# Feed-forward down products: two row tiles at a time by seven block products instead of eight

## The chip, the cores and the metric

The kernel runs on one core of one Trainium2 chip. The time is the device time of one execution, in microseconds (us). Three runs of the kernel before took 1896.27, 1896.74 and 1897.19 us; their median is 1896.74 us.

## What is computed

256 tokens (two tiles of 128) of width 1024 pass through fourteen stages: eight gated feed-forward layers and six other stages (a pooling mixer, the shared latent keys and values, latent attention, a norm, a mixer of stick-breaking attention and convolution, gated linear attention). Only the feed-forward layers matter here:

```
swiglu(u, wg, wu, wd) = (silu(u @ wg) * (u @ wu)) @ wd        # u 256x1024, wg and wu 1024x2816, wd 2816x1024
```

The hidden width of 2816 is 22 tiles of 128 (`NF`). Everything is float32. The kernel gets the precision out of TensorE by splitting each operand into a rounded high part and the rest (`hi` and `lo`, both in the fp32r format), and it computes each product as three: hi by hi, hi by lo and lo by hi.

## The kernel before, in words

A feed-forward stage (`ffn`, in each engine's program) runs over 22 steps, one per tile of the hidden width. Step f has two parts on TensorE:

- **gate and up** (`gate_up`, `block_of`): 8 blocks of the width by 3 products by 2 (gate, up) = 48 matmuls of 256 columns, into two PSUM banks of `X`; steps alternate between banks 0, 1 and banks 2, 3.
- **down** (`down`, `down_half`): the hidden tile of 128 rows (2 token tiles) against 1024 columns of `wd` (2 halves): 4 banks of `Y` by 3 products = 12 matmuls of 512 columns (one of them in two halves of 256). `Y` gathers all 22 steps.

TensorE runs gate and up of step f, then down of step f-1. All matmuls go through the helper at L1698.

The weights come from memory by SyncE's queue, in order: one 1 MB tile A (gate and up) and one 0.5 MB tile B (down) per step, each double buffered. `load_A` (L401) waits until the tile before last is split, `load_B` (L406) likewise. ScalarE makes the high parts (`split_A` L590, 2048 columns; `split_B` L610, 1024 columns), VectorE the low parts by a subtraction of two SBUF operands (L1105, L1117). Between these, each step has its activation: VectorE scales gate and up by the norm's root out of PSUM (L1257, L1260), ScalarE applies silu (L708), VectorE multiplies (L1267), ScalarE and VectorE split the product (L717, L1270). One stage (`ffn2`, "reuse") needs no scaling and reads gate and up straight from PSUM. The order of each engine's queue is written out by hand in `step`; the last steps are peeled.

At a stage's end `following` starts the next stage's transposes, VectorE adds Y into the residual (`update`; L1176 where there is no second norm). The next stage's first A tiles are split in the last steps: tile a+22 belongs to the next stage. GpSimd has almost nothing to do: powers for the norms (L475, L489) and a few DMAs and memsets.

Of the kernel before, what the change touches and what calls it, by code (L numbers as in the profile page):

```python
# [16 lines left out]
P = 128  # L17
# [9 lines left out]
POOL_REACH = P + 16  # L27
GLA_HEADS, GLA_DV = 4, 256
# [74 lines left out]
def build(nc, wa, wb, x, cols_in, rows_in, ident_in, trig_in, pool_in, penal_in, sb_in, gla_in, gate_in, taps_in,  # L103
# [8 lines left out]
    with ctx:  # L112
# [8 lines left out]
        rawB = [sb(f"rawB{i}", [P, 1024]) for i in range(2)]  # L121
        hiA = [sb(f"hiA{i}", [P, 2048], f32r) for i in range(2)]
        loA = [sb(f"loA{i}", [P, 2048], f32r) for i in range(2)]
        hiB = [sb(f"hiB{i}", [P, 1024], f32r) for i in range(2)]
        loB = [sb(f"loB{i}", [P, 1024], f32r) for i in range(2)]
# [12 lines left out]
        act_s = sb("act_s", [P, 2, TOKENS])  # L138
        act_h = sb("act_h", [P, 2, TOKENS])
        act_hh = sb("act_hh", [P, 2, TOKENS], f32r)  # L140
        act_hl = sb("act_hl", [P, 2, TOKENS], f32r)
# [9 lines left out]
        cqh = sb("cqh", [P, 2, TOKENS], f32r)  # L151
        cql = sb("cql", [P, 2, TOKENS], f32r)
# [56 lines left out]
        root = arena[:, 12000:12000 + TOKENS]  # L209
# [29 lines left out]
        s_mask = s_const[:, 4 * P:4 * P + 384]  # L239
        s_k = rg.take(SB_PAIRS, TOKENS)  # L240
        s_q = rg.take(SB_PAIRS, 2, TOKENS)
# [8 lines left out]
        s_w = rg.take(4, 384)  # L250
# [6 lines left out]
        g_mask = rg.take(8 * P)  # L257
        g_qk = rg.take(GLA_HEADS, 512)
# [8 lines left out]
        g_sm = rg.take(8, P)  # L267
# [37 lines left out]
        out_done = sem("out_done")  # L305

# [50 lines left out]

        def tap(c, j):
            w = COL["conv_w"] + CONV_W * c + j
            return s_pad[:, c, j:j + TOKENS], cols[:, w:w + 1]  # L360
# [30 lines left out]

        HALF = [slice(0, 512), slice(512, 1024)]
# [3 lines left out]
        def _(sp):  # L396
# [6 lines left out]
            def load_B(n, p, first=False):  # L403
                if not first:
                    sp.wait_ge(b_lo, n - 1)
                sp.dma_start(rawB[p][:, :], wb[n]).then_inc(b_loaded[p], 16)  # L406
# [9 lines left out]
            for s in plan:  # L416
                a, b = s["a"], s["b"]
                if s["kind"] == "ffn":
                    peel = 2 if a == 0 else 0
                    for f in range(peel):  # L420
                        if f == 0:
                            load_A(a + 1, (a + 1) % 2, first=True)
                        load_B(b + f, (b + f) % 2, first=True)
                        if f == 0:
                            sp.dma_start(cols[:, KD:NCOL], cols_in[:, KD:NCOL]).then_inc(const_loaded, 16)
                    with sp.Fori(peel // 2, NF // 2) as j:
                        for p in range(2):
                            load_A(a + p + 2 * j, (a + p) % 2)
                            load_B(b + p + 2 * j, (b + p) % 2)
# [23 lines left out]
        def _(pool):  # L453
# [18 lines left out]
            for s in plan:  # L472
# [20 lines left out]
                before_mixer = {"ffn1": ("mla",), "final": ("hyb",), "ffn5": ("gla",)}.get(s["name"], ())  # L493
                if s["late"]:
# [7 lines left out]
                if s["a"] == 0:  # L502
                    load_row(0)
                    pool.wait_ge(a_hi, 4)
# [5 lines left out]
                for k in before_mixer:  # L510
# [15 lines left out]
                    if k == "gla":  # L526
                        pool.wait_ge(a_hi, s["a"] + 8)
                        pool.dma_start(arena[:, 0:20 * P], gla_in).then_inc(phase_loaded[k], 16)
                        pool.dma_start(g_gate, gate_in).then_inc(phase_loaded[k], 16)
                        nc.gpsimd.memset(g_lr[0:32, :], 1.0).then_inc(g_ones, 1)  # L530
                if s["kind"] == "kv":
# [39 lines left out]
        def _(act):  # L571
# [90 lines left out]
            def ffn(s):  # L662
# [29 lines left out]
                split_B(b, b % 2)  # L692

                def step(f, p, first=False, last=False):
                    if first:
                        if a:
                            split_A(a + 2, a % 2, 0)
                        if s["late"]:
                            act.wait_ge(root_psum, s["deferred"] + 1)
                            nc.scalar.activation(root, Y[:, 0, 0:TOKENS], ACT.Copy).then_inc(root_done, 1)  # L700
                        if s["reuse"]:
                            latent_root()
# [2011 lines left out]
```

## Time and profile before

| | us |
|---|---|
| median of three runs (lowest to highest) | 1896.74 (1896.27 to 1897.19) |
| span of the profiled execution, first to last instruction | 1894.6 |
| TensorE busy in it | 1874.1 (99%) |
| VectorE busy | 1229.6 (65%) |
| ScalarE busy | 945.6 (50%) |
| GpSimd busy | 66.1 (3%) |
| moved by DMA | 338.6 MB, 179 GB/s on average |

The profiled execution has its span alone; what lies around it is taken as the difference to the median of the runs, 2.1 us. TensorE's mean granted clock is 0.999. A busy share says how much of the span an engine executed something; the chain that ended last says which engine everything else waited for. In the rows below PE is TensorE's matmuls, DVE is VectorE, ACT is ScalarE, POOL is GpSimd.

### The profile page before, as it was taken

What the parts mean: (1) busy time and instruction counts of PE and PEld (TensorE: products, weight loads), DVE (VectorE), ACT (ScalarE), POOL (GpSimd) and SP (SyncE); (2) the same over time, 40 slices, a digit from 0 to 9 for tenths busy, and PEclk for the clock granted to TensorE, in tenths of its full rate; (3) what the DMA queues carried; (4) which work ended last, traced back from release to release, by engine and by line L of the source; (5) the groups of instructions that cost most, each with busy time, mean ns of one, the idle gap of its engine ahead of it and who ended that gap; (6) DMA issues with size and microseconds to landing.
All of it is one profiled execution on the core that took longest, in us unless ns stands there. A gap on an engine that the chain in (4) does not pass through costs nothing.

```text
span 1894.6 us, 34284 instructions
## 1 busy us (share of the span) xinstructions
PE 1874.1 (99%) x13508; PEld 1745.4 (92%) x13508; DVE 1229.6 (65%) x1654; ACT 945.6 (50%) x1301; POOL 66.1 (3%) x94
## 2 busy tenths in 40 slices
PE   9999999999999999999999999999999999999998
PEld 8999999999998889999999998999999998889998
DVE  5666765675556647666765699765676665877665
ACT  5444544454446636444544457644454446455443
POOL 0000100000000000000100000100010002010000
PEclk9999999999999999999999999999999999999999
DMA  7555455545453245555555443565545453344552
GB/s 282 199 191 184 164 199 199 189 165 207 185 198 134 68 149 215 191 183 194 200 199 198 146 145 111 201 233 199 189 167 203 185 199 126 130 152 178 192 199 100
DMA packets 61505, 338.60 MB, mean 179 GB/s; under 512 B 6976, under 2 KB 7360, under 8 KB 33024
## 3 DMA queue, kind: packets, MB, share of 16 engines
q1 hardware_dynamic: 59472, 330.00, 47.3%
q0 software_dynamic: 1968, 7.70, 1.2%
q8 instruction: 45, 0.74, 0.2%
q14 instruction: 20, 0.16, 0.0%
HBM read 336.62 MB, written 1.05 MB: 178 GB/s over the span
## 4 chain that ended last, share of the span: by engine, by line
PE 93%; DVE 3%; ACT 2%; issue 1%; POOL 1%; DMA 1%; SPq 0%; DVEq 0%; ACTq 0%; POOLq 0%
PE X L1698 55%; PE Y L1698 36%; DMA rawA<-in_wa 1%; ACT hiA L590 1%; PE X L1739 1%; ACT arena L804 0%; DVE arena L1481 0%; DVE xs L1193 0%; DVE h L1200 0%; DVE xl L1145 0%; PE Y L2213 0%; DVE loA L1105 0%; DVE arena L1418 0%; POOL ms_eps L489 0%; PE X L1722 0%
## 5 line engine op out<-in xcount | busy, mean ns | idle before, releaser
L1698 PE MATMUL X<-xh,hiA 128*128 128x256 f32 x2464 | 679.0, 277 | 1.7 <-DVE loA L1091 0.8
L1698 PE MATMUL X<-xl,hiA 128*128 128x256 f32 x2464 | 677.4, 277 | 0.0
L1698 PE MATMUL X<-xh,loA 128*128 128x256 f32 x2464 | 668.9, 277 | 0.0
L1105 DVE TENSOR_TENSOR loA<-rawA,hiA 128x2048 fp32r<-128x2048 f32 x213 | 487.9, 2290 | 265.2 <-ACT hiA L590 265.0
L1698 PEld LDWEIGHTS X<-xh,hiA 128*128 128x128 f32 x2464 | 462.7, 188 | 3.2 <-DVE loA L1091 1.7
L1698 PEld LDWEIGHTS X<-xl,hiA 128*128 128x128 f32 x2464 | 463.3, 188 | 0.0
L1698 PEld LDWEIGHTS X<-xh,loA 128*128 128x128 f32 x2464 | 457.1, 188 | 0.0
L590 ACT ACTIVATE hiA<-rawA 128x2048 fp32r<-128x2048 f32 (+1 forms) x239 | 424.0, 1776 | 46.1 <-PE Y L1698 29.8
L708 ACT ACTIVATE act_s<-act_s 128x256 f32<-128x256 f32 x154 | 64.4, 418 | 427.2 <-DVE act_s L1257 427.2
L1698 PE MATMUL Y<-hiB,act_hh 128*128 128x512 f32 x704 | 275.5, 391 | 0.9 <-DVE act_hl L1270 0.9
L1698 PE MATMUL Y<-hiB,act_hl 128*128 128x512 f32 (+1 forms) x880 | 275.9, 346 | 0.0
L1698 PE MATMUL Y<-loB,act_hh 128*128 128x512 f32 x704 | 275.0, 391 | 0.0
L1117 DVE TENSOR_TENSOR loB<-rawB,hiB 128x1024 fp32r<-128x1024 f32 x180 | 219.3, 1218 | 3.9 <-ACT hiB L610 3.8
L717 ACT ACTIVATE act_hh<-act_h 128x256 fp32r<-128x256 f32 x176 | 73.5, 417 | 284.7 <-DVE act_h L1267 284.7
L1698 PEld LDWEIGHTS Y<-hiB,act_hl 128*128 128x128 f32 x880 | 165.2, 188 | 35.3
L610 ACT ACTIVATE hiB<-rawB 128x1024 fp32r<-128x1024 f32 x181 | 189.1, 1045 | 1.6 <-PE Y L1698 1.5
L1260 DVE TENSOR_TENSOR act_h<-X,arena 128x256 f32<-128x256 f32 x148 | 62.5, 423 | 150.7 <-PE X L1698 150.7
L1698 PEld LDWEIGHTS Y<-hiB,act_hh 128*128 128x128 f32 x704 | 132.2, 188 | 24.6 <-issue 3.3
L1698 PEld LDWEIGHTS Y<-loB,act_hh 128*128 128x128 f32 x704 | 132.2, 188 | 21.1
L1270 DVE TENSOR_TENSOR act_hl<-act_h,act_hh 128x256 fp32r<-128x256 f32 x176 | 74.8, 425 | 85.5 <-ACT act_hh L717 85.5
L1698 PE MATMUL X<-oh,hiA 128*128 128x256 f32 x352 | 97.6, 277 | 0.0
L1698 PE MATMUL X<-ol,hiA 128*128 128x256 f32 x352 | 97.4, 277 | 0.0
(263 smaller groups left out, 2217.8 us busy)
## 6 DMA issues: line engine op xcount, KB each, us to landing
rawA<-in_wa SPq DMA_DIRECT2D x221, 1024.0 KB, 5.4
rawB<-in_wb SPq DMA_DIRECT2D x181, 512.0 KB, 3.5
row_gain<-in_rows POOLq DMA_DIRECT2D x8, 512.0 KB, 6.1
arena<-in_gla POOLq DMA_DIRECT2D x1, 1280.0 KB, 5.8
h<-in_x SPq DMA_DIRECT2D x2, 512.0 KB, 4.0
arena<-in_taps POOLq DMA_DIRECT2D x1, 576.0 KB, 5.7
arena<-in_pool POOLq DMA_DIRECT2D x1, 544.0 KB, 6.6
rawA<-in_wa SPq DMA_DIRECT2D x2, 256.0 KB, 5.9
```

The source lines that it names most:

```text
L590: ins = nc.scalar.activation(hiA[p][:, cut], rawA[p][:, cut], ACT.Copy)
L610: nc.scalar.activation(hiB[p][:, :], rawB[p][:, :], ACT.Copy).then_inc(b_hi, 1)
L708: nc.scalar.activation(act_s[:, p, :], act_s[:, p, :], ACT.Silu).then_inc(silu_done, 1)
L717: nc.scalar.activation(act_hh[:, p, :], act_h[:, p, :], ACT.Copy).then_inc(prod_hi, 1)
L1105: nc.vector.tensor_tensor(loA[p][:, :], rawA[p][:, :], hiA[p][:, :].bitcast(f32), ALU.subtract).then_inc(a_lo, 1)
L1117: nc.vector.tensor_tensor(loB[p][:, :], rawB[p][:, :], hiB[p][:, :].bitcast(f32), ALU.subtract).then_inc(b_lo, 1)
L1260: nc.vector.tensor_tensor(act_h[:, p, :], up, root, ALU.mult).then_inc(up_scaled, 1)
L1270: nc.vector.tensor_tensor(act_hl[:, p, :], act_h[:, p, :], act_hh[:, p, :].bitcast(f32), ALU.subtract).then_inc(prod_lo, 1)
L1698: return say(nc.tensor.matmul(*args, **kw))
L1739: ins = nc.tensor.transpose(dst, src, ident[:, :])
```

## The change

In nine of the eleven pairs of steps (`PAIRS = 9`, the first 18 tiles) the down part of two steps is one product of 2 by 2 blocks (2 token tiles by 2 hidden tiles) with 2 by 2 blocks (2 hidden tiles by 2 column halves). It is done with seven block products in place of eight. This needs four sums of weight blocks (u1 to u4, `sums`) and four sums of activation blocks (r3, s1, s2, r4), which GpSimd makes, and seven PSUM banks (Y0 to Y3, X0 to X2) that are joined once, after the ninth pair, on ScalarE and VectorE. The last four tiles run as before (`left`). Gate and up of a step share one bank now: X3 (X2 for f = 1). The weight buffers rawB, sum_hi and sum_lo hold a pair (2048 columns). `taken` takes gate and up (512 columns) out of PSUM in one instruction. The high and low parts of three raw blocks (1536 columns), of the four weight sums (2048) and of the eight activation blocks (1024) replace the splits of B and of the product. The order of the matmuls: gate and up of 2j, `first_sums(j-1)` (9 matmuls of 512 columns), gate and up of 2j+1, `last_sums(j-1)` (12).

```diff
 # SyncE
+                    def pair_loads(j):
+                        load_A(a + 1 + 2 * j, (a + 1) % 2)
+                        load_A(a + 2 + 2 * j, a % 2)
+                        sp.wait_ge(w_sum_done, pairs + j)
+                        sp.wait_ge(b_lo, b + 2 * j)
+                        for p in range(2):
+                            sp.dma_start(rawB[(b + p) % 2], wb[b + p + 2 * j]).then_inc(b_loaded[(b + p) % 2], 16)
...
+                    load_A(a + NF - 1, (a + NF - 1) % 2)
+                    load_B(b + NF - 2, b % 2)
+                    load_B(b + NF - 1, (b + 1) % 2)
 # GpSimd
+                def weight_sums(j):
...
+                    pool.wait_ge(w_sum_lo, pairs + j)
...
+                    nc.gpsimd.tensor_tensor(sums[:, 0:1024].rearrange("p (a b) -> p a b", b=512), ends, twice, ALU.add
+                                            ).then_inc(w_sum_part, 1)
+                    pool.wait_ge(w_sum_part, 2 * (pairs + j) + 1)
...
+                    nc.gpsimd.tensor_tensor(sums[:, 1024:1536], u3, weight_block(s, "b11"), ALU.add
+                                            ).then_inc(w_sum_part, 1)
+                    pool.wait_ge(w_sum_part, 2 * (pairs + j) + 2)
+                    nc.gpsimd.tensor_tensor(sums[:, 1536:2048], sums[:, 1024:1536], weight_block(s, "b21"), ALU.add
+                                            ).then_inc(w_sum_done, 1)
+                def product_sums(j):
+                    pool.wait_ge(prod_done, NF * s["ffn"] + 2 * j + 2)
+                    blocks = prod.rearrange("p (a b) -> p a b", b=P)
+                    nc.gpsimd.tensor_tensor(blocks[:, 4:6, :], blocks[:, 1:2, :].broadcast_to([P, 2, P]),
+                                            blocks[:, 0:4:3, :], ALU.subtract).then_inc(p_sum_part, 1)
+                    pool.wait_ge(p_sum_part, 2 * (pairs + j) + 1)
+                    nc.gpsimd.tensor_tensor(blocks[:, 6, :], blocks[:, 5, :], blocks[:, 0, :], ALU.subtract
+                                            ).then_inc(p_sum_part, 1)
+                    pool.wait_ge(p_sum_part, 2 * (pairs + j) + 2)
+                    nc.gpsimd.tensor_tensor(blocks[:, 7, :], blocks[:, 2, :], blocks[:, 6, :], ALU.add
+                                            ).then_inc(p_sum_done, 1)
 # ScalarE, the loop and what follows it
+                with act.Fori(1, PAIRS) as j:
+                    product_parts(j - 1)
+                    sum_parts(j - 1)
+                    silu(2 * j, 0)
+                    split_A(a + 2 * j + 2, a % 2)
+                    raw_parts(j)
+                    silu(2 * j + 1, 1)
+                    split_A(a + 2 * j + 3, (a + 1) % 2)
...
+                split_A(a + f + 4, a % 2)
+                silu(f + 3, 1)
+                left_product(3)
 # VectorE
+                def taken(f, p):
...
+                    dve.wait_ge(up_psum, e + 1 + f)
+                    if s["late"]:
+                        wide = root.rearrange("p (a b) -> p a b", a=1).broadcast_to([P, 2, TOKENS])
+                        ins = nc.vector.tensor_tensor(act_sh[:, :, p, :], bank, wide, ALU.mult)
...
+                    ins.then_inc(gate_scaled, 1)
...
+                product(0, 0)
...
+                split_A(a + 2, a % 2)
+                taken(1, 1)
+                raw_low(0)
+                product(1, 1)
+                split_A(a + 3, (a + 1) % 2)
+                with dve.Fori(1, PAIRS) as j:
+                    product_low(j - 1)
+                    sum_low(j - 1)
+                    taken(2 * j, 0)
+                    product(2 * j, 0)
+                    split_A(a + 2 * j + 2, a % 2)
+                    raw_low(j)
+                    taken(2 * j + 1, 1)
+                    product(2 * j + 1, 1)
+                    split_A(a + 2 * j + 3, (a + 1) % 2)
+                f = 2 * PAIRS
...
+                nc.vector.tensor_tensor(Y[:, 1, :], Y[:, 1, :], sums[:, 512:1024], ALU.subtract).then_inc(joint_chain, 1)
...
+                left_product_low(1)
+                left_weights_low(1)
+                taken(f + 2, 0)
...
+                left_weights_low(3)
+                split_A(a + f + 4, a % 2)
+                taken(f + 3, 1)
 # TensorE
-                        pe.wait_ge(prod_done, e - 1 + f)
+                        pe.wait_ge(gate_scaled, e + f)
...
+                def first_sums(j, first=False, last=False):
+
+                    pe.wait_ge(b_lo, b + 2 * j + 2)
+                    pe.wait_ge(p_sum_lo, pairs + j + 1)
+                    joined(X[:, 0, :], prod_block("a11"), raw_block(s, "b11"), first, last)
+                    joined(Y[:, 0, :], prod_block("a12"), raw_block(s, "b21"), first, last)
+                    return joined(Y[:, 1, :], prod_block("r4"), raw_block(s, "b22"), first, last, True).then_inc(b_free, 2)
+
+                def last_sums(j, first=False, last=False):
+
+                    pe.wait_ge(w_sum_lo, pairs + j + 1)
+                    joined(Y[:, 2, :], prod_block("a22"), sum_block(s, "u4"), first, last)
+                    joined(Y[:, 3, :], prod_block("s1"), sum_block(s, "u1"), first, last)
+                    joined(X[:, 1, :], prod_block("s2"), sum_block(s, "u2"), first, last)
+                    joined(X[:, 2, :], prod_block("r3"), sum_block(s, "u3"), first, last, True).then_inc(all_sums_psum, 1)
...
-                down(0, 0, first=True)
-                with pe.Fori(1, NF // 2 - 1) as j:
+                gate_up(2, 0)
+                first_sums(0, True)
+                gate_up(3, 1)
+                last_sums(0, True)
+                with pe.Fori(2, PAIRS) as j:
                     gate_up(2 * j, 0)
-                    down(2 * j - 1, 1)
+                    first_sums(j - 1)
                     gate_up(2 * j + 1, 1)
-                    down(2 * j, 0)
+                    last_sums(j - 1)
```

`joined` is three matmuls of 512 columns (the third in two halves where it is told so). For the stages whose first B tile has an even number, the host swaps the column halves of the even tiles of the pairs. Some arena regions move so that `prod` and `sums` are free in all stages. No other stage's instructions change.

## Rows read from the trace of the kernel before

**Rows 1.** The page: busy time of each engine, and the chain that ended last, by line.

```profile
PE 1874.1 (99%) x13508; PEld 1745.4 (92%) x13508; DVE 1229.6 (65%) x1654; ACT 945.6 (50%) x1301; POOL 66.1 (3%) x94
...
PE X L1698 55%; PE Y L1698 36%; DMA rawA<-in_wa 1%; ACT hiA L590 1%; PE X L1739 1%; ACT arena L804 0%; DVE arena L1481 0%; DVE xs L1193 0%; DVE h L1200 0%; DVE xl L1145 0%; PE Y L2213 0%; DVE loA L1105 0%; DVE arena L1418 0%; POOL ms_eps L489 0%; PE X L1722 0%
```

**Rows 2.** Busy time by engine in 18 steps of stage ffn1 (columns in the first row).

```profile
core 0: us, PE busy (x) PEld busy (x) DVE busy (x) ACT busy (x) POOL busy (x), PEclk, DMA share, GB/s
227.60:375.20 147.60, 147.60 (x1101) 139.63 (x1100) 93.05 (x111) 65.06 (x73) 0.00 (x0) 1.00 0.53 196
```

**Rows 3.** Chain of waits of stage ffn1: start us, us, what; its opening, then its end.

```profile
208.72 5.23 PE Y L1698 x46
...
219.97 2.75 PE Y L1698 x13
222.72 5.46 PE X L1698 x48
...
383.98 5.70 PE Y L1698 x26
```

**Rows 4.** Groups of instructions, every shape apart: TensorE, VectorE and ScalarE in the steps.

```profile
L1698 PE MATMUL Y<-hiB,act_hh 128*128 128x512 f32 x704 | 275.5, 391 | 0.9 <-DVE act_hl L1270 0.9
...
L1105 DVE TENSOR_TENSOR loA<-rawA,hiA 128x2048 fp32r<-128x2048 f32 x213 | 487.9, 2290 | 265.2 <-ACT hiA L590 265.0
L1117 DVE TENSOR_TENSOR loB<-rawB,hiB 128x1024 fp32r<-128x1024 f32 x180 | 219.3, 1218 | 3.9 <-ACT hiB L610 3.8
L590 ACT ACTIVATE hiA<-rawA 128x2048 fp32r<-128x2048 f32 x203 | 386.4, 1903 | 40.9 <-PE Y L1698 29.8 <-PE X L1698 9.5 <-PE X L1739 0.7
L610 ACT ACTIVATE hiB<-rawB 128x1024 fp32r<-128x1024 f32 x181 | 189.1, 1045 | 1.6 <-PE Y L1698 1.5
L708 ACT ACTIVATE act_s<-act_s 128x256 f32<-128x256 f32 x154 | 64.4, 418 | 427.2 <-DVE act_s L1257 427.2
L1267 DVE TENSOR_TENSOR act_h<-act_s,act_h 128x256 f32<-128x256 f32 x154 | 65.4, 425 | 13.8 <-DVE act_h L1260 8.1 <-issue 1.4
L1176 DVE SCALAR_TENSOR_TENSOR h<-Y,h 128x512 f32<-128x512 f32 x24 | 16.4, 690 | 12.8 <-PE Y L1698 12.7
```

**Rows 5.** Timeline of VectorE over one step (start us, us, engine, line, operation, idle before).

```profile
1074.27 2.29 DVE L1105 TENSOR_TENSOR loA<-rawA,hiA 128x2048 fp32r<-128x2048 f32 x1 [1.38 <-ACT hiA L590]
...
1079.29 0.42 DVE L1260 TENSOR_TENSOR act_h<-X,arena 128x256 f32<-128x256 f32 x1 [1.26 <-PE X L1698]
1079.75 0.42 DVE L1267 TENSOR_TENSOR act_h<-act_s,act_h 128x256 f32<-128x256 f32 x1
```

**Rows 6.** Groups of instructions on GpSimd.

```profile
L523 POOL MEMSET arena<- 128x2048 f32 x1 | 1.8, 1835 | 0.0
L519 POOL MEMSET k_rope<- 128x512 f32 x1 | 0.5, 514 | 0.0
L525 POOL CAST mask_r<-arena 128x128 fp32r<-128x128 f32 x1 | 0.3, 291 | 0.8 <-DMA arena<-in_sb 0.8
L544 POOL TENSOR_TENSOR token_var<-rstd 128x2 f32<-128x2 f32 x1 | 0.2, 207 | 0.0
```

**Rows 7.** Timelines of GpSimd and VectorE where the two meet, and where GpSimd is alone.

```profile
193.89 0.56 POOL L475 TENSOR_TENSOR rstd<-ms_eps,minus_half 128x1 f32<-128x1 f32 x1
...
907.30 2.54 POOL L475 TENSOR_TENSOR rstd<-ms_eps,minus_half 128x1 f32<-128x1 f32 x1 [2.05 <-DVE ms_eps L1123]
...
907.13 2.28 DVE L1105 TENSOR_TENSOR loA<-rawA,hiA 128x2048 fp32r<-128x2048 f32 x1
909.39 1.22 DVE L1117 TENSOR_TENSOR loB<-rawB,hiB 128x1024 fp32r<-128x1024 f32 x1
...
214.82 1.31 DVE L1117 TENSOR_TENSOR loB<-rawB,hiB 128x1024 fp32r<-128x1024 f32 x1
```

**Rows 8.** DMA issues: size each, median us from issue to landing.

```profile
rawA<-in_wa SPq DMA_DIRECT2D x221, 1024.0 KB, 5.4
rawB<-in_wb SPq DMA_DIRECT2D x181, 512.0 KB, 3.5
```

More of the change, by code:

```diff
@@ L526, in _ @@
                     if k == "gla":
+                        for j in range(3):
+                            weight_sums(j)
+                            product_sums(j)
                         pool.wait_ge(a_hi, s["a"] + 8)
@@ L530, in _ @@
                         nc.gpsimd.memset(g_lr[0:32, :], 1.0).then_inc(g_ones, 1)
+                if s["kind"] == "ffn":
+                    if s["a"]:
+                        wait_h_all(pool, s)
+                    for j in range(3 if "gla" in before_mixer else 0, PAIRS):
+                        if j or s["a"]:
+                            weight_sums(j)
+                        product_sums(j)
                 if s["kind"] == "kv":
@@ L691, in ffn @@
                     token_square(1)
[L692 to L702, printed above, removed]
-                        split_A(a + 2, a % 2, 1 if a else 0)
-                    else:
-                        split_B(b + f, (b + p) % 2)
-                    if s["late"]:
-                        act.wait_ge(gate_scaled, NF * s["deferred"] + 1 + f)
+                pairs = PAIRS * s["ffn"]
@@ new lines, in raw_parts, with sum_parts @@
+                def raw_parts(j):
+                    for p in range(2):
+                        n = b + p + 2 * j
+                        act.wait_ge(b_loaded[n % 2 if isinstance(n, int) else (b + p) % 2], loads(n, (b + p) % 2))
+                    act.wait_ge(b_free, b + 2 * j + 2)
+                    skip = weight_places(s)[1]
+                    nc.scalar.activation(raw_halves(s)[0], rawB_pair[:, skip:skip + 1536], ACT.Copy).then_inc(b_hi, 2)
+                def sum_parts(j):
+                    act.wait_ge(w_sum_done, pairs + j + 1)
+                    act.wait_ge(all_sums_psum, pairs + j)
+                    nc.scalar.activation(sum_hi[:, :], sums, ACT.Copy).then_inc(w_sum_hi, 1)
@@ new lines, in sum_low, with product_low @@
+                def sum_low(j):
+                    dve.wait_ge(w_sum_hi, pairs + j + 1)
+                    nc.vector.tensor_tensor(sum_lo[:, :], sums, sum_hi[:, :].bitcast(f32), ALU.subtract
+                                            ).then_inc(w_sum_lo, 1)
+                def product_low(j):
+                    dve.wait_ge(p_sum_hi, pairs + j + 1)
+                    nc.vector.tensor_tensor(prod_hl[:, :], prod, prod_hh[:, :].bitcast(f32), ALU.subtract
+                                            ).then_inc(p_sum_lo, 1)
@@ new lines, in ffn @@
+                sum_low(PAIRS - 1)
+                taken(f, 0)
+                product(f, 0)
+                split_A(a + f + 2, a % 2)
+                left_weights_low(0)
+                left_product_low(0)
+                dve.wait_ge(joint_copied, 2 * s["ffn"] + 1)
+                nc.vector.tensor_tensor(Y[:, 0, :], Y[:, 0, :], sums[:, 0:512], ALU.add).then_inc(bank_joined, 1)
+                taken(f + 1, 1)
+                product(f + 1, 1)
+                split_A(a + f + 3, (a + 1) % 2)
@@ L2634, in lay_out @@
             wa.append(np.stack([column_tiles(g), column_tiles(u)], 2))
-            wb.append(d.reshape(NF, P, D))
+            rows = d.reshape(NF, P, 2, 512)
+            if not sum(len(t) for t in wb) % 2:
+                rows = np.concatenate([rows[n:n + 1, :, ::-1] if n < 2 * PAIRS and n % 2 == 0 else rows[n:n + 1]
+                                       for n in range(NF)])
+            wb.append(rows.reshape(NF, P, D))
         if kind == "pool":
```

351 lines of the change are left out of this document (247 added, 104 removed).

## The prediction, made before the changed kernel ran

> **What bounds the kernel now.** I read the page first: TensorE is busy 99% of the span, and the chain that ended last lies to 91% in its matmuls into X and Y [rows 1]. Next the window over 18 steps of one stage: 147.60 of 147.60 us are TensorE at the full granted clock, VectorE is busy for 93.05, ScalarE for 65.06, GpSimd for nothing [rows 2]. That is 8.20 us a step, 16.40 a pair. The chain splits it: 5.46 us for 48 matmuls of gate and up, 2.75 for the 13 of a down part [rows 3]; so 512 columns take 0.228 us. (The 391 ns of one such matmul in the groups [rows 4] overlap with the next.) Last the slack: before the scaling of up, VectorE waits 1.26 us per step for TensorE, and before the low part of A another 1.38 for ScalarE [rows 5]. Only the first is spare. The second is a serial chain (product, high part, low part), which matters once VectorE gets more.
>
> **TensorE.** Each of the 9 pairs does 21 instead of 24 down matmuls: 27 x 0.228 = 6.2 us less per stage, 49 over eight stages. A pair becomes 16.40 - 0.68 = 15.7 us. This is the whole gain; all else can only cost.
>
> **VectorE and ScalarE in the pair loop, nobody disturbing.** Instructions of 2048 columns take 2.29 us on VectorE, of 1024 1.22, of 256 0.42 [rows 4]; 1536 lies between, 1.75; 512 out of PSUM takes 0.69, as L1176 does. Per pair VectorE has two A low parts, raw_low 1.75, product_low 1.22, sum_low 2.29, two taken, two products: 12.1 us busy, against 10.4 before. To this its waits come. After each taken: silu 0.42, then ScalarE's high part 1.90, then the low part 2.29. I walk it (neighbours overlap by 0.08, a semaphore costs 0.03): 0.69 + 0.03 + 0.42 + 1.81 + 0.04 + 2.21 = 5.2 per step, twice, plus 1.67 + 1.14 + 2.21 = 15.4 us. That is just under the 15.7 of TensorE: the loop would stay TensorE's, with 0.3 us to spare. ScalarE (two high parts of A, 1.47 raw, 1.90 sums, 1.04 product, two silu: 9.1) fits. Of the loads, B of the next pair is issued when raw_low ends and the sums are made, and has some 8 us until the weight sums need it; 3.5 us to land [rows 8] fit.
>
> **What GpSimd costs.** Per pair it adds 2048 columns for the weights (1024, 512, 512) and 512 for the products (256, 128, 128). The trace has no long addition on it. Memsets of 512 and 2048 columns differ by 1.32 us: 0.86 ns a column for one written stream. The cast of 128 columns took 0.29, some 1.5 ns a column with a read. Two columns of an addition took 0.21 in all [rows 6]. So the bounds are 0.86 ns a column (all streams overlap) and 2.58 (none does), with 0.1 to 0.2 fixed. I take 2.1, nearest to the cast plus a second read in part, and 0.1 fixed. The weight sums are then 2.25 + 1.18 + 1.18 = 4.6 us, the product sums 0.64 + 0.37 + 0.37 = 1.4. The Trainium skill (GPSIMD Engine Reference, section Performance versus the Vector engine) has 4497 ns for an addition of 2048 columns; by it the sum would stay within 1 us per stage of mine.
>
> **Who shares with GpSimd.** Alone, a power of one column takes GpSimd 0.56 us; begun during the low part of A at 907.13, the same took 2.54, and ended 0.4 after it [rows 7]. So GpSimd stands still while VectorE subtracts two SBUF operands. What VectorE loses behind a long GpSimd instruction no row shows. The bounds: nothing (its 2.28 and 1.22 there are undisturbed, though GpSimd only wanted one column), or the whole instruction, the same rule turned round. A low part of B that began 0.1 us behind a DMA issue of GpSimd took 1.31, not 1.22. I take the whole, by symmetry. With nothing, only the waits of GpSimd count (rival 3). The skill (SBUF — State Buffer, section Who interferes with whom) speaks against this change: a VectorE instruction with two SBUF inputs and a GpSimd instruction that reads SBUF exclude each other, whichever starts first. The rows agree for one direction; by that rule the time is my forecast's, by the row alone rival 3's.
>
> Now 10.7 us of two-SBUF work on VectorE (two A low parts, raw, sum and product lows, two products) and 6.0 on GpSimd exclude each other: 16.7 us in a pair. The walk, from the end of an even taken at 0: the first weight sum began with it at -0.5 and ends at 1.75, so the product slips from 0.45 to 1.75 (hidden, the high part ends at 2.25); the second sum goes from 2.15 to 3.33, so the low part of A slips by **1.05**; the third waits behind back-to-back low parts until 7.3 and runs beside taken; in the second half the three product sums run in the wait for the high part and push the low part by **0.34**. Period 15.4 + 1.05 + 0.34 = 16.8, against 16.4 before. TensorE waits 1.05 per pair.
>
> **The stage's start.** Down(0) stood between step 1 and step 2 as cover. Without it, gate and up of 2 waits for taken(1), which is queued behind product(0) and the low part of A: 1.7 to 2.2 us. First_sums(0) waits for the new chain product(1), product sums, high, low: 0.5, or 2.7 if the product sums get stuck behind a low part. Gate and up of 3 waits for sum_low(0) and taken(2): 1.4. **The end.** The join (six instructions of 0.69 on VectorE, two copies on ScalarE) fits under gate and up of 20 except for 0.5 to 1.3. The loads: B 21 now waits for a low part queued behind the join, and in SyncE's queue the next stage's A 22 waits behind B 21. It lands some 6 us after (5.4 alone [rows 8]), and its high and low parts stand ahead of silu(21) and taken(21): 2.8 us. Before, nothing of this was seen; the end ran as 5.70 us of matmuls without a gap [rows 3].
>
> **Sum per stage:** 2.2 + 2.7 + 1.4 at the start, 8 x 1.05 in the loop, 1.3 + 2.8 at the end = 18.8 us of waits, less 6.2: +12.6. By eight: 101. Against the profiled execution's 1894.6 this gives 1995, and with the 2.1 us to the median and less in the last stage, which has no next tile (-2.8), 1995 on the scale of the runs. Nothing below 0.2% (3.8 us) counts as a difference.
>
> **Rivals.**
> 1. *As forecast, but the third product sum misses its gap.* Two sums and their semaphores (0.09 each) take 1.2 us after the product; the low part of A is due 1.4 after it. The forecast has the third sum in by 0.2 us. With 0.15 or more fixed per instruction, it waits out a low part (2.2 us), ScalarE's product and sum parts follow late, sum_low and taken with them: period 18.9, stage +30, in all **2137**. For: the addition of two columns took 0.21. Against: the memsets' fixed part is 0.07.
> 2. *No exclusion that costs, or additions near 0.86 ns.* Then the loop is TensorE's at 15.7, waits 7.0 per stage, less 6.2: +0.8, **1903**.
> 3. *Only GpSimd waits.* The product sums come later at the start, the loop holds: +2.5 per stage, **1917**; if the third sum misses, period 17.7, **2050**.
> 4. *Faster.* The loop at 15.7 and less than half of the 7 us at start and end: the decisive place is A 22 at the end, which costs nothing if it lands 2.8 us earlier, and the opening, where the chain of taken(1) would have to be hidden. With 2.5 us of waits per stage, 8 x (2.5 - 6.2) = -30, **1867**. For: TensorE is the bound and gets less work. Against: the row of a blocked GpSimd, and VectorE's chain with 0.3 us to spare.
>
> That the change doesn't do what it says is no rival: the matmuls are fewer by count.
>
> **Chances.** Forecast 0.38 (its own range 1950 to 2030, by 1.7 to 2.2 ns a column), rival 1 with the late form of 3 0.25 (2040 to 2200), rivals 2 and 3 0.20 (1895 to 1950; within 0.2% 0.06), rival 4 0.17. The range 1888 to 2150 leaves out most of rival 4 and the slow end of rival 1. Slower: 0.38 + 0.25 + 0.14 = 0.77.
>
> **What would show it.** Right: TensorE's busy time in a pair near 15.7 while the pair takes 16.8; gaps before gate and up of odd steps, of about 0.75 us, whose releaser is taken; A low parts of 2.29 us that start after GpSimd's sum rather than after ScalarE; GpSimd instructions much longer than alone; gaps of 2 to 3 us at steps 2, 3 and 21. Wrong: pairs of 15.7 us, or low parts running beside a GpSimd addition at full speed.

## The result and the profile after

The changed kernel takes 2192.69 us, median of four runs (2190.79 to 2194.34), beside 1896.51 us for the kernel before on the same chip (1895.84 to 1897.19). The ratio is 1.156, with a 95% interval of 1.155 to 1.158: 296 us slower. The forecast was slower, by 101 us; the measured time lies beyond its range of 1888 to 2150 us.

The page of the changed kernel, busy time of each engine and the chain by line:

```profile
PE 1910.4 (87%) x13292; PEld 1744.0 (80%) x13292; DVE 1635.3 (75%) x1513; ACT 1061.7 (48%) x1245; POOL 825.8 (38%) x526
...
PE Y L1971 11%; DVE ol L1454 8%; POOL arena L596 8%; ACT sum_hi L824 6%; PE X L1971 6%; DVE act_sh L1438 4%; ACT oh L818 4%; DVE loA L1286 3%; ACT hiA L706 3%; POOL arena L590 3%; DMA rawA<-in_wa 3%; POOL arena L593 2%; DVE arena L1446 2%; ACT act_sh L858 2%; DVE xl L1454 1%
```

TensorE has 216 matmuls fewer and is no longer the bound. In [rows 1] matmuls into X and Y held 91% of the chain, here 17%. The rest goes round VectorE (25%), ScalarE (17%) and GpSimd (13%), and 23% is "issue", time in which the engine named waited for nothing that the profile shows. The window of six pairs of stage ffn1 (columns in its first row) shows the same:

```profile
core 0: us, PE busy (x) PEld busy (x) DVE busy (x) ACT busy (x) POOL busy (x), PEclk, DMA share, GB/s
280.00:398.32 118.32, 99.92 (x717) 91.53 (x716) 91.29 (x55) 52.10 (x43) 64.41 (x37) 1.00 0.46 160
```

A pair is 118.32 / 6 = 19.72 us, against 16.40 before [rows 2]. TensorE is idle for 3.1 us of each. The clock is full in the loop, so these are waits, not a slower TensorE. Measured from the start of one matmul to the start of the next, less their usual distance (0.12 us for 256 columns, 0.23 for 512), a pair has waits of 1.8, 1.3 and 0.6 us, with 0.1 us more behind each: 4.0 us, the difference to the 15.72 us of an undisturbed pair (first experiment). TensorE's waits are given in this way from here on; they are some 0.16 us longer than the idle time of the trace. What stands behind them, the groups say (out of PSUM is `taken`, L1438; `product` L1446; `raw_low` L1454; GpSimd's weight sums L575, L579, L582 and product sums L590, L593, L596):

```profile
L1286 DVE TENSOR_TENSOR loA<-rawA,hiA 128x2048 fp32r<-128x2048 f32 x213 | 558.0, 2620 | 175.1 <-ACT hiA L706 171.7
L582 POOL TENSOR_TENSOR arena<-arena,rawB 128x512 f32<-128x512 f32 x72 | 222.6, 3091 | 5.6
L1454 DVE TENSOR_TENSOR ol<-rawB,oh 128x1536 fp32r<-128x1536 f32 x63 | 172.9, 2744 | 0.0
L575 POOL TENSOR_TENSOR arena<-rawB 128x1024 f32<-128x1024 f32 x72 | 172.5, 2396 | 348.6 <-DVE sum_lo L1460 348.5
L596 POOL TENSOR_TENSOR arena<-arena 128x128 f32<-128x128 f32 x72 | 167.5, 2326 | 5.6
L1446 DVE TENSOR_TENSOR arena<-act_sh 128x256 f32<-128x256 f32 x176 | 163.9, 931 | 82.3 <-ACT act_sh L858 81.5 <-ACT act_sh L861 0.8
...
L1438 DVE TENSOR_TENSOR act_sh<-X,arena 128x512 f32<-128x512 f32 x147 | 100.0, 680 | 0.5 <-PE X L1971 0.5
L579 POOL TENSOR_TENSOR arena<-arena,rawB 128x512 f32<-128x512 f32 x72 | 98.8, 1372 | 5.6
L830 ACT ACTIVATE prod_hh<-arena 128x1024 fp32r<-128x1024 f32 x72 | 76.2, 1059 | 205.3 <-POOL arena L596 205.3
```

Two instructions of one shape give it away: the second and third weight sum both add 512 columns, and take 1.37 and 3.09 us. The third product sum adds 128 columns in 2.33 us. On VectorE the multiplication of 256 columns takes 0.93 us on average instead of 0.43 [rows 4]. These are waits written down as work, for both engines. So VectorE's 75% on the page is no measure of its work. The place of each is in one pair of the timelines of VectorE, then GpSimd:

```profile
317.74 0.68 DVE L1438 TENSOR_TENSOR act_sh<-X,arena 128x512 f32<-128x512 f32 x1
318.90 1.76 DVE L1446 TENSOR_TENSOR arena<-act_sh 128x256 f32<-128x256 f32 x1 [0.48 <-ACT act_sh L858]
320.71 3.25 DVE L1286 TENSOR_TENSOR loA<-rawA,hiA 128x2048 fp32r<-128x2048 f32 x1
323.89 2.84 DVE L1454 TENSOR_TENSOR ol<-rawB,oh 128x1536 fp32r<-128x1536 f32 x1
326.66 0.68 DVE L1438 TENSOR_TENSOR act_sh<-X,arena 128x512 f32<-128x512 f32 x1
327.82 0.42 DVE L1446 TENSOR_TENSOR arena<-act_sh 128x256 f32<-128x256 f32 x1 [0.48 <-ACT act_sh L858]
329.63 2.29 DVE L1286 TENSOR_TENSOR loA<-rawA,hiA 128x2048 fp32r<-128x2048 f32 x1 [1.39 <-ACT hiA L706]
333.45 1.23 DVE L1466 TENSOR_TENSOR prod_hl<-arena,prod_hh 128x1024 fp32r<-128x1024 f32 x1 [1.52 <-ACT prod_hh L830]
335.25 2.29 DVE L1460 TENSOR_TENSOR sum_lo<-arena,sum_hi 128x2048 fp32r<-128x2048 f32 x1 [0.58 <-ACT sum_hi L824]
337.46 0.68 DVE L1438 TENSOR_TENSOR act_sh<-X,arena 128x512 f32<-128x512 f32 x1
```

```profile
317.99 2.39 POOL L575 TENSOR_TENSOR arena<-rawB 128x1024 f32<-128x1024 f32 x1 [5.46 <-DVE sum_lo L1460]
320.46 1.36 POOL L579 TENSOR_TENSOR arena<-arena,rawB 128x512 f32<-128x512 f32 x1
321.90 3.22 POOL L582 TENSOR_TENSOR arena<-arena,rawB 128x512 f32<-128x512 f32 x1
328.32 0.74 POOL L590 TENSOR_TENSOR arena<-arena 128x256 f32<-128x256 f32 x1 [3.20 <-DVE arena L1446]
329.14 0.47 POOL L593 TENSOR_TENSOR arena<-arena 128x128 f32<-128x128 f32 x1
329.69 2.56 POOL L596 TENSOR_TENSOR arena<-arena 128x128 f32<-128x128 f32 x1
```

Read them against each other. The product begun at 318.90 ends at 320.66, 0.28 us behind the first weight sum. The low part of A begun at 320.71 ends 2.14 us behind the second sum, about its own length. The third sum, begun at 321.90, waits for this low part (until 323.96) and then runs *before* raw_low, although that was next in VectorE's queue without a gap: raw_low takes 2.84 us instead of 1.75. The third product sum begins 0.06 us behind the low part of 329.63 and ends 0.33 us behind it. ScalarE's product and sum parts and VectorE's product_low and sum_low (1.52 and 0.58 us of waits) are late by that. The product and the first weight sum read different tiles (`act_sh`, `rawB`), so it is not one tile that they contend for. The pattern stands in every pair but the first of each stage; there the third product sum takes 0.46 us and raw_low 1.74 to 2.22.

By stage, the eight feed-forward stages grew by 44.0, 36.9, 36.0, 36.1, 37.1, 36.7, 36.6 and 34.9 us, 298 in all; all others stayed within 0.2 us. In ffn1 TensorE waits for 2.9, 1.8 and 1.3 us at the start, 0.9 and 2.0 at the end.

### The profile page after: what moved, and what is told of

It is laid out like the page before. It is cut to its first block, busy times and chain, and to the rows that moved or that the text cites. A ratio compares the mean times of both kernels' runs of the same rounds, so it can differ in the third digit from the quotient of the medians.

```text
span 2192.5 us, 32913 instructions
## 1 busy us (share of the span) xinstructions
PE 1910.4 (87%) x13292; PEld 1744.0 (80%) x13292; DVE 1635.3 (75%) x1513; ACT 1061.7 (48%) x1245; POOL 825.8 (38%) x526
## 3 DMA queue, kind: packets, MB, share of 16 engines
HBM read 336.62 MB, written 1.05 MB: 154 GB/s over the span
## 4 chain that ended last, share of the span: by engine, by line
DVE 25%; issue 23%; PE 18%; ACT 17%; POOL 13%; DMA 3%; ACTq 1%; DVEq 0%; SPq 0%; POOLq 0%
PE Y L1971 11%; DVE ol L1454 8%; POOL arena L596 8%; ACT sum_hi L824 6%; PE X L1971 6%; DVE act_sh L1438 4%; ACT oh L818 4%; DVE loA L1286 3%; ACT hiA L706 3%; POOL arena L590 3%; DMA rawA<-in_wa 3%; POOL arena L593 2%; DVE arena L1446 2%; ACT act_sh L858 2%; DVE xl L1454 1%
## 5 line engine op out<-in xcount | busy, mean ns | idle before, releaser
L858 ACT ACTIVATE act_sh<-act_sh 128x256 f32<-128x256 f32 x175 | 72.9, 417 | 684.5 <-DVE act_sh L1438 599.1
L575 POOL TENSOR_TENSOR arena<-rawB 128x1024 f32<-128x1024 f32 x72 | 172.5, 2396 | 348.6 <-DVE sum_lo L1460 348.5
L1446 DVE TENSOR_TENSOR arena<-act_sh 128x256 f32<-128x256 f32 x176 | 163.9, 931 | 82.3 <-ACT act_sh L858 81.5
L582 POOL TENSOR_TENSOR arena<-arena,rawB 128x512 f32<-128x512 f32 x72 | 222.6, 3091 | 5.6
L1460 DVE TENSOR_TENSOR sum_lo<-arena,sum_hi 128x2048 fp32r<-128x2048 f32 x72 | 165.1, 2293 | 41.4 <-ACT sum_hi L824 41.4
L830 ACT ACTIVATE prod_hh<-arena 128x1024 fp32r<-128x1024 f32 x72 | 76.2, 1059 | 205.3 <-POOL arena L596 205.3
L1466 DVE TENSOR_TENSOR prod_hl<-arena,prod_hh 128x1024 fp32r<-128x1024 f32 x72 | 88.2, 1225 | 115.9 <-ACT prod_hh L830 115.9
L1454 DVE TENSOR_TENSOR ol<-rawB,oh 128x1536 fp32r<-128x1536 f32 x63 | 172.9, 2744 | 0.0
L596 POOL TENSOR_TENSOR arena<-arena 128x128 f32<-128x128 f32 x72 | 167.5, 2326 | 5.6
L590 POOL TENSOR_TENSOR arena<-arena 128x256 f32<-128x256 f32 x72 | 58.5, 812 | 231.2 <-DVE arena L1446 231.2
L824 ACT ACTIVATE sum_hi<-arena 128x2048 fp32r<-128x2048 f32 x72 | 136.4, 1894 | 0.0
```

The source lines that it names most:

```text
L575: nc.gpsimd.tensor_tensor(sums[:, 0:1024].rearrange("p (a b) -> p a b", b=512), ends, twice, ALU.add).then_inc(w_sum_part, 1)
L582: nc.gpsimd.tensor_tensor(sums[:, 1536:2048], sums[:, 1024:1536], weight_block(s, "b21"), ALU.add).then_inc(w_sum_done, 1)
L590: nc.gpsimd.tensor_tensor(blocks[:, 4:6, :], blocks[:, 1:2, :].broadcast_to([P, 2, P]), blocks[:, 0:4:3, :], ALU.subtract).then_inc(p_sum_ ...
L596: nc.gpsimd.tensor_tensor(blocks[:, 7, :], blocks[:, 2, :], blocks[:, 6, :], ALU.add).then_inc(p_sum_done, 1)
L824: nc.scalar.activation(sum_hi[:, :], sums, ACT.Copy).then_inc(w_sum_hi, 1)
L858: nc.scalar.activation(act_s[:, p, :], act_s[:, p, :], ACT.Silu).then_inc(silu_done, 1)
```

## The experiments

Theory 1: an addition of GpSimd (it reads SBUF) and a VectorE instruction with two SBUF inputs exclude each other, whichever begins first, and six additions in a serial chain meet VectorE at the wrong places. First rival: GpSimd's time and its chain of semaphores alone are too long. Second rival: GpSimd's writes to the same buffers slow VectorE.

### Additions that read nothing

```diff
-nc.gpsimd.tensor_tensor(sums[:, 0:1024]..., ends, twice, ALU.add).then_inc(w_sum_part, 1)
+nc.gpsimd.memset(sums, 0.0).then_inc(w_sum_part, 1)
 # the other five likewise: sums[:, 0:1536] twice, prod[:, 512:1024] three times
```

> The changed kernel with GpSimd's six additions per pair replaced by six memsets of about the same total length (2048, 1536 and 1536 columns for the weight sums, three of 512 for the product sums; by the memsets of the kernel before 1.83 + 1.4 + 1.4 us and 3 x 0.51 us, against 2.39 + 1.36 + about 1.3 and 0.74 + 0.46 + 0.46 for the additions when nothing holds them). All waits, places and semaphores stay. The block sums are left out, so four of the seven block products are of zeros. Theory 1 (an addition of GpSimd that reads SBUF and a VectorE instruction with two SBUF inputs keep each other out): memsets read nothing, so VectorE's product takes 0.43 us and its low part of A 2.29 us again, no GpSimd instruction takes over 1.9 us, the pair comes down from 19.72 us to 15.7 to 16.0 us, and the whole to 1895 to 1925 us (start and end waits of 5 to 8 us per stage against 6.2 us saved). Rival A (GpSimd's own time and the chain of semaphores through it make the wait, whoever shares a port): the pair stays at 18.5 us or more and the time at 2130 us or more. Rival B (the write traffic to the same buffers is what slows VectorE): low parts of A stay near 2.6 us on average, the pair at 17 to 18 us, the time 1990 to 2070 us.

This kernel leaves out the sums, so it prices the additions and doesn't compute the layer. Measured: 1905.44 us (1904.32 to 1906.48), ratio to the kernel before 1.005 (1.003 to 1.006). Three pairs in a window, then GpSimd's and VectorE's timeline over the same places as above:

```profile
280.00:327.16 47.16, 47.16 (x359) 44.85 (x358) 35.39 (x27) 26.12 (x22) 18.51 (x19) 1.00 0.56 199
```

```profile
318.27 1.81 POOL L575 MEMSET arena<- 128x2048 f32 x1 [5.46 <-DVE sum_lo L1454]
320.14 1.39 POOL L578 MEMSET arena<- 128x1536 f32 x1
321.58 1.38 POOL L580 MEMSET arena<- 128x1536 f32 x1
```

```profile
319.21 0.43 DVE L1440 TENSOR_TENSOR arena<-act_sh 128x256 f32<-128x256 f32 x1 [0.49 <-ACT act_sh L852]
321.03 2.29 DVE L1280 TENSOR_TENSOR loA<-rawA,hiA 128x2048 fp32r<-128x2048 f32 x1 [1.39 <-ACT hiA L700]
323.24 1.75 DVE L1448 TENSOR_TENSOR ol<-rawB,oh 128x1536 fp32r<-128x1536 f32 x1
```

GpSimd is busy for 6.2 us of a pair beside the same instructions (six undisturbed additions take 6.7), and nobody waits for it. The pair is 15.72 us, TensorE's own, and TensorE fills it. Both rivals fall. Of the 296 us, 287 go when the additions become writes alone. Of the 10 us by which it is behind the kernel before, nearly all are in the first stage (9.6 us longer than before, by the loads: below). In the others the waits at start and end, 5.9 us in ffn1, use up the 6.2 us saved: they differ from the kernel before by 0.6 us at most, but for the last, which is 1.4 us shorter.

### The third product sum let in

```diff
                     product(2 * j + 1, 1)
+                    dve.wait_ge(p_sum_done, pairs + j + 1)
                     split_A(a + 2 * j + 3, (a + 1) % 2)
```

> The changed kernel with one wait more: in each pair VectorE waits for the third product sum (p_sum_done) before it starts the low part of the odd A tile, so that this sum is not shut out by that low part. Theory 1 (the third sum misses its gap by less than 0.1 us and then waits out the low part): the third product sum falls from 2.33 us to about 0.46 us, VectorE gives up 0.4 to 0.5 us for it, ScalarE's product and sum parts start about 2 us earlier, and the pair goes from 19.72 to 18.0 to 18.3 us; nine pairs by eight stages make 72 x 1.6 = 115 us, so about 2078 us (2060 to 2100). Rival (ScalarE or the weight sums set the pair and the third product sum is late beside something as late): less than 30 us gained, or VectorE's added wait costs its 0.5 us per pair, 2160 to 2230 us.

Measured: 2078.01 us (2077.30 to 2080.08), the theory's number. A wait *added* to VectorE gains 115 us. The pair is 18.08 us, so the third product sum was worth 1.64 us of 19.72. Its row:

```profile
L596 POOL TENSOR_TENSOR arena<-arena 128x128 f32<-128x128 f32 x72 | 33.0, 459 | 5.6
```

### The third weight sum held back

```diff
                     pool.wait_ge(w_sum_part, 2 * (pairs + j) + 2)
+                    pool.wait_ge(b_lo, s["b"] + 2 * j + 2)
```

> The kernel of e2 (VectorE waits for the third product sum ahead of the low part) with one wait more: GpSimd holds the third weight sum back until raw_low has ended, so that it can't get in between two low parts that follow each other. This is the walk of the prediction made true: third product sum in its gap, third weight sum behind raw_low. Theory 1 (each of the two is a step that the forecast put wrongly, and nothing else is): raw_low falls from 2.74 to 1.75 us, the pair from 18.1 to 16.8 to 17.0 us, 72 pairs x 1.1 to 1.3 = 79 to 94 us less than the 2078 us of e2: 1984 to 2000 us. Rival (the third weight sum pays elsewhere what it no longer costs there: it pushes the product of the odd step, or ScalarE's sum parts come too late): 2050 to 2080 us.

This is on top of the wait just added. Measured: 2022.24 us (2020.59 to 2022.99): 56 us less, where 79 to 94 were expected, and no rival's number either. The pair is 17.19 us. Raw_low is down to 1.75 us as expected, but the pair is still 0.4 us over the walk. VectorE's timeline from the low part of the even step on, GpSimd's, and ScalarE's high part of the odd A tile:

```profile
309.56 3.26 DVE L1287 TENSOR_TENSOR loA<-rawA,hiA 128x2048 fp32r<-128x2048 f32 x1
312.74 1.75 DVE L1455 TENSOR_TENSOR ol<-rawB,oh 128x1536 fp32r<-128x1536 f32 x1
314.41 0.68 DVE L1439 TENSOR_TENSOR act_sh<-X,arena 128x512 f32<-128x512 f32 x1
315.57 0.63 DVE L1447 TENSOR_TENSOR arena<-act_sh 128x256 f32<-128x256 f32 x1 [0.48 <-ACT act_sh L859]
318.22 2.29 DVE L1287 TENSOR_TENSOR loA<-rawA,hiA 128x2048 fp32r<-128x2048 f32 x1 [2.01 <-POOL arena L597]
```

```profile
314.63 1.29 POOL L583 TENSOR_TENSOR arena<-arena,rawB 128x512 f32<-128x512 f32 x1 [3.97 <-DVE ol L1455]
316.29 0.74 POOL L591 TENSOR_TENSOR arena<-arena 128x256 f32<-128x256 f32 x1 [0.36 <-DVE arena L1447]
317.10 0.46 POOL L594 TENSOR_TENSOR arena<-arena 128x128 f32<-128x128 f32 x1
317.64 0.45 POOL L597 TENSOR_TENSOR arena<-arena 128x128 f32<-128x128 f32 x1
```

```profile
315.45 1.90 ACT L707 ACTIVATE hiA<-rawA 128x2048 fp32r<-128x2048 f32 x1
```

The third weight sum (to 315.92) runs beside taken, which has one operand in PSUM and isn't held (0.68 us), but it holds the product by 0.2. From the end of the product (316.20) to the low part of A (318.22) the three product sums with their semaphores take 2.02 us, where the walk had 1.74 (a gap of 1.4 and 0.34 beyond it). ScalarE is done at 317.35, so with the walk's 0.04 behind it the low part is pushed by 0.82 us, not 0.34: 0.2 by the late product, 0.28 by the longer sums. In the even step the low part takes 3.26 us, 0.97 more than undisturbed, where the walk had 1.05. Together 0.48 - 0.08 = 0.4 us: with these two put right the walk gives the measured pair.

### The product sums on VectorE

```diff
+                    product_sums(j)      # VectorE, three additions
                     split_A(a + 2 * j + 3, (a + 1) % 2)
 # GpSimd
-                        product_sums(j)
```

> The changed kernel with the three product sums on VectorE (they stand right behind the second product, in the wait for the high part of A) and the weight sums still on GpSimd. Theory 1: the three additions take VectorE about 0.42 + 0.3 + 0.3 us in a gap of 1.4 us that it has there, the low part of A stays where it was, and product and sum parts start 2 us or more earlier; the weight sums still hold VectorE's product by 1.3 us and a low part of A by 1.0 us, and the third still gets in between two low parts for 1.1 us. Pair 17.5 to 18.0 us, time 2192 - 72 x 2.0 = 2050 us (2020 to 2080). Rival (the weight sums alone make nearly all of the loss): the pair stays above 19 us, 2130 us or more. Rival 2 (the product sums made nearly all of it): pair 16 us, 1930 us or less.

Measured: 2026.33 us (2025.58 to 2027.09), pair 17.45 us. The time is within the expectation, the pair 0.05 us below it. The weight sums alone still cost 17.45 - 15.72 = 1.7 us per pair.

### All six sums on VectorE

```diff
 # VectorE; GpSimd makes none
                     product_low(j - 1)
-                    sum_low(j - 1)
                     taken(2 * j, 0)
                     product(2 * j, 0)
+                    sum_low(j - 1)
                     split_A(a + 2 * j + 2, a % 2)
                     raw_low(j)
                     taken(2 * j + 1, 1)
                     product(2 * j + 1, 1)
+                    product_sums(j)
+                    weight_sums(j)
                     split_A(a + 2 * j + 3, (a + 1) % 2)
```

> The changed kernel with all six sums on VectorE: product sums and then weight sums right behind the second product, and sum_low moved behind the product of the even step; GpSimd does none of them. Theory 1 (mutual exclusion is the loss, not the amount of elementwise work): additions of 1024, 512, 512, 256, 128 and 128 columns on VectorE cost 1.22 + 0.7 + 0.7 + 0.42 + 0.25 + 0.25 = 3.5 us, of which about 2.8 us lie in VectorE's waits for ScalarE's high parts; VectorE is then busy 15.5 us in a pair, TensorE needs 15.7, and the pair takes 15.7 to 16.2 us. With 5 to 8 us of start and end waits per stage against 6.2 us saved: 1890 to 1930 us. Rival (VectorE's serial chain with ScalarE does not fit the 3.5 us in): pair 17 to 18 us, 1990 to 2070 us.

Measured: 1998.61 us (1995.55 to 2001.35). The expectation missed by 70 us; the time is in the range of its rival, the pairs of 16.6 to 16.8 us lie below the rival's 17 to 18. VectorE has the time, but product_low comes too late in its queue. TensorE's first matmul of `first_sums` waits for it in each pair:

```profile
L1962 PE MATMUL X<-oh,prod_hh 128*128 128x512 f32 x63 | 31.7, 504 | 55.4 <-DVE prod_hl L1453 55.4
```

From the trace it is a ring: from `taken` of the odd step to the end of product_low 8.7 us of VectorE (product, six additions, low part of A, product_low), then 8.1 us of TensorE until gate and up of the next odd step are there (first_sums, gate and up). Together 16.8, whatever the engines have free elsewhere. In this order 0.72 us of each pair are TensorE's wait, with 0.1 more behind it.

### Product_low ahead of the low part of A

```diff
                 with dve.Fori(1, PAIRS) as j:
-                    product_low(j - 1)
                     taken(2 * j, 0)
-                    product(2 * j, 0)
                     sum_low(j - 1)
+                    product(2 * j, 0)
                     split_A(a + 2 * j + 2, a % 2)
                     raw_low(j)
                     taken(2 * j + 1, 1)
+                    weight_sum_a(j)      # the 1024 columns, in the wait for silu
                     product(2 * j + 1, 1)
                     product_sums(j)
-                    weight_sums(j)
+                    weight_sums_bc(j)
+                    product_low(j)
                     split_A(a + 2 * j + 3, (a + 1) % 2)
```

> All six sums on VectorE as in e4, in another order, so that product_low of a pair stands ahead of the low part of the odd A tile and not behind it, and VectorE's two waits for silu are filled (sum_low in the first, the sum of 1024 columns in the second). In e4 the pair took 16.8 us because of a ring: product_low (8.7 us of VectorE's work behind taken) lets first_sums start, and 8.1 us later TensorE gives the next gate and up to taken. Theory: with product_low 2.2 us earlier TensorE is the bound again: pair 15.7 to 15.9 us, and with waits of 5.5 to 7 us per stage at start and end (and some 7 us once in the first stage) 1885 to 1912 us. Rival (VectorE's total, 15.2 us of a pair by e4's durations, doesn't fit in with its waits for ScalarE): pair 16.2 us or more, 1930 us or more.

Measured: 1900.97 us (1898.80 to 1902.98, ten runs), ratio 1.003 (1.002 to 1.004), as expected. The pair is 15.72 us. The same row and VectorE's timeline over a pair:

```profile
L1967 PE MATMUL X<-oh,prod_hh 128*128 128x512 f32 x63 | 25.2, 400 | 5.7 <-DVE prod_hl L1456 5.7
```

```profile
312.47 0.69 DVE L1392 TENSOR_TENSOR act_sh<-X,arena 128x512 f32<-128x512 f32 x1 [0.27 <-PE X L1967]
...
319.99 0.69 DVE L1392 TENSOR_TENSOR act_sh<-X,arena 128x512 f32<-128x512 f32 x1 [0.42 <-PE X L1967]
...
328.19 0.69 DVE L1392 TENSOR_TENSOR act_sh<-X,arena 128x512 f32<-128x512 f32 x1 [0.26 <-PE X L1967]
```

VectorE now waits for TensorE, 0.7 us of 15.72, and for nothing else. The six sums that made the kernel 292 us longer on GpSimd (2192.7 against 1901.0) fit into VectorE's own queue. The time is now the kernel before's but for 5 us: what the loop gains, start and end give back.

### The loads alone

```diff
                     load_B(b + NF - 2, b % 2)
+                    if a + NF < total["a"]:
+                        load_A(a + NF, a % 2)   # and not again at the next stage's start
                     load_B(b + NF - 1, (b + 1) % 2)
```

> The changed kernel with SyncE's order alone changed: the next stage's first A tile is issued ahead of the last B tile instead of behind it. It prices the wait at the end of a stage. Theory: the 2.0 us before the last down part go in the six stages that another feed-forward or mixer tile follows, and in the first stage the 5.9 us that VectorE waited for this tile with what TensorE lost to its low clock there: 15 to 25 us less than 2192.7 us: 2168 to 2178 us. Rival (the last B tile, issued later, takes the A tile's place as the wait): 2185 to 2195 us.

Measured, on the changed kernel: 2175.08 us (2174.68 to 2176.33), 17.6 us less, as expected. The first stage gives 8.6 of them, most others some 2. In the changed kernel's first stage VectorE, whose queue held the weighting of the pooling's A tile (L1347), stood still for the tile behind the last B:

```profile
222.06 2.29 DVE L1347 TENSOR_TENSOR rawA<-rawA,row_gain 128x2048 f32<-128x2048 f32 x1 [5.94 <-DMA rawA<-in_wa]
```

### Start and end mended

```diff
 # VectorE, on top of the order above, and of the loads
+                raw_low(0)                       # ahead of the scaling of step 0
...
+                if a:
+                    split_A(a + 2, a % 2)
                 product(0, 0)
...
 # TensorE
-                        pe.wait_ge(gate_scaled, e + f)
+                        pe.wait_ge(gate_scaled, e + 1 if isinstance(f, int) and f == 2 else e + f)
```

> e6 with start and end mended: gate and up of step 2 waits for taken(0) alone (their bank has no other reader), raw_low(0) moves ahead of the scaling of step 0 and the low part of A ahead of product(0), and SyncE issues the next stage's first A tile ahead of the last B tile. Theory: of the 1.8 us before step 2 some 0.4 are left, of those before the sums of pair 0 and step 3 about 1.9 together, and at the end 0.6 in place of 2.1 to 2.9, so 2.9 us of waits against 6.2 us saved: 3.3 us less than the kernel before in each of eight stages, 1870 us (1860 to 1885). Rival (the loads, with 22 A tiles and 22 B tiles in less time, or the turned order at start and end, bring a new wait as long): 1885 to 1905 us.

Measured: 1872.73 us (1872.58 to 1873.15), as expected, ratio to the kernel before 0.988 (0.986 to 0.989): 23 us less than the kernel before and 320 less than the changed one. Its page:

```profile
PE 1836.8 (98%) x13292; PEld 1710.1 (91%) x13292; DVE 1622.9 (87%) x1945; ACT 1069.3 (57%) x1245; POOL 69.8 (4%) x94
```

In ffn1 four waits of 0.44, 0.51, 0.65 and 0.46 us are left, and the stage takes 179.6 us against 183.0: 6.2 saved, 2.1 in waits, and 0.7 that no wait of TensorE in the loop accounts for.

## Why the prediction was wrong in size and right in direction

By its own steps:

- **TensorE: right.** 15.7 us a pair forecast; 15.72 in the first and sixth experiments, with TensorE without a gap.
- **VectorE and ScalarE undisturbed: right.** The loop holds at 15.72 when GpSimd only writes.
- **GpSimd's rate: nearly right.** 2.25 and 1.18 us forecast for 1024 and 512 columns; 2.40 and 1.37 measured (1.29 where nothing runs beside it). The small ones were mis-sized: 0.64, 0.37 and 0.37 us forecast, 0.74, 0.46 and 0.46 measured. The fixed part was put at 0.1 us; 128 and 256 columns differ by 0.28 us, which leaves 0.18.
- **Exclusion both ways: right.** It was taken by symmetry, without a row, so that was a guess that held. The product held for 1.76 us and the free one at 0.42, and the first experiment, show it. The Trainium skill (SBUF — State Buffer, section Who interferes with whom) says of the GpSimd side that an instruction which reads SBUF contends with a VectorE instruction of two SBUF inputs, and one that only writes doesn't. Here both halves hold: 0.43 us for the product beside a memset, 1.76 beside an addition.
- **"The forecast has the third sum in by 0.2 us": the step that failed.** The walk had the third product sum begun 1.2 us after the product, the low part of A due at 1.4. It began 1.45 us after it (328.24 to 329.69) and missed by 0.06. The fixed part of 0.18 is rival 1's own condition ("0.15 or more"), and rival 1's mechanism is what happened. Its price, shown by the second experiment, is 1.64 us a pair, some 115 us of the 198 between forecast and result.
- **"The third waits behind back-to-back low parts until 7.3 and runs beside taken": failed.** It gets in between them, and raw_low pays. The third experiment prices it at 0.89 us a pair, some 56 us, with the third product sum already let in. The one row that bears on it spoke against it: in [rows 7] the power begun at 907.30 ended at 909.84, inside the second of two low parts (with one instruction of 0.15 us between them, which [rows 7] leaves out). The assumption made the forecast's walk, and rival 1's too, so that even rival 1 (18.9 us a pair, 2137 us) stopped short of 19.72.
- **Product sums push the low part by 0.34: mis-sized.** 0.82, by the longer sums and by the product that the third weight sum holds. With the even step's 0.97 in place of 1.05 it leaves 0.4 us a pair, and 27 us in all (2022.2 - 1995; start and end lie in that too). So the pair is 16.8 + 0.4 + 0.9 + 1.6 = 19.7. The last two are differences of runs, so that this sum closes is no proof; the 0.4 was found in the timeline.
- **Start and end: right but for the first stage.** 10.4 us of waits forecast beside the loop (2.2, 2.7, 1.4, 1.3, 2.8), 8.9 measured in ffn1 (2.9, 1.8, 1.3, 0.9, 2.0). A tile 22 landing late was foreseen; that in the first stage VectorE's queue waits for it directly (L1347), 8.6 us, was not.
- **The range.** Rival 1 had a range of its own, 2040 to 2200 us, and the measured time lies in it. The stated range ended at 2150. The first failed step alone led to rival 1's 2137, within it; only with the second does the time leave it.
- **Rivals 2 and 3** (no exclusion, or only GpSimd waits) are out. **Rival 4**, faster, was right about the place: with the loop at 15.7 and start and end nearly hidden the time is 1872.7 us, beside the 1867 worked out for it. But that takes GpSimd out of the change.

What stays open: which waits of TensorE lower its clock, when GpSimd gets in between two VectorE instructions (both below), and the last 0.7 us of ffn1 in the final version.

## What to carry to other kernels

GpSimd is not a second VectorE where VectorE works on two SBUF operands. Count the time of such VectorE instructions and of GpSimd's that read SBUF as one sum, and then count the places where they meet: an instruction that misses a gap by 0.06 us waits for a whole neighbour, in every iteration. When an instruction's mean time is above that of its twin of the same shape, look for what it waits for; the engine's busy share is then no measure of its load. Before moving work off an engine, look for its idle time in other places of its own queue, follow the ring from the work back to itself over all engines, and put at the front what another engine waits for.

## What was not expected of the hardware

- GpSimd can get in between two VectorE instructions that follow each other at once: the third weight sum, begun during a low part, ran ahead of raw_low in 64 of the 72 pairs, all but the first of each stage (raw_low then 2.84 us, against 1.75 undisturbed). VectorE's record of raw_low starts as if nothing had happened (323.89) and includes the wait. It is no rule. In the kernel before, a small GpSimd instruction that began 0.55 us ahead of the end of one low part waited out the next too. The third weight sum had begun 2.1 us ahead. What decides this stays open. VectorE, then GpSimd, in the kernel before:

```profile
1578.71 1.23 DVE L1117 TENSOR_TENSOR loB<-rawB,hiB 128x1024 fp32r<-128x1024 f32 x1 [0.46 <-ACT hiB L610]
1579.86 2.28 DVE L1105 TENSOR_TENSOR loA<-rawA,hiA 128x2048 fp32r<-128x2048 f32 x1
```

```profile
1579.39 2.84 POOL L489 TENSOR_SCALAR ms_eps<-ms 128x1 f32<-128x1 f32 x1 [7.01 <-ACT xs L613]
```

- The lengths are those of a VectorE that is held and then runs at full speed: what the product, the low part and raw_low take beyond their own time is the rest of GpSimd's instruction to within 0.15 us (the low part: 3.25 - 2.29 = 0.96, and the second sum had 1.11 us to go at 320.71).
- Where a stage starts or ends with longer waits, TensorE's clock may fall. The granted clock was at its lower level (1.2 instead of 2.4 GHz) for 49.3 us in ten stretches of the changed kernel, against one of 4.9 us before and one of 4.2 in the final version. The longest, 10.2 us at the end of the first stage, began behind a wait of 2.2 us and took in one of 2.6 us; the window over it (columns as above):

```profile
226.50:237.00 10.50, 8.07 (x22) 5.95 (x21) 6.18 (x8) 4.42 (x8) 0.72 (x2) 0.52 0.51 200
```

The waits in the loop, 1.8, 1.3 and 0.6 us in each pair, did not lower it (1.00 in the window of six pairs). Which waits do was not tried apart.
